# GpSimd's half of a weight split ahead of the seventh conditioning load, and 64-row products of attention in pairs on two row groups

## The reference

```python
hh = modulate(rmsnorm(x, g_pre), m[0], m[1])
f = swiglu(hh, w_ffn_gate, w_ffn_up, w_ffn_down)
x = x + 0.5 * m[2] * rmsnorm(f, g_post)
```

```python
att = einsum('bihd,bjhd->bhij', qb, kb) * decay
inner = einsum('bhij,bjhv->bihv', att, vb)
cross = einsum('bihd,bhdv->bihv', qb, s) * q_dec
s = s * c_dec + einsum('bjhd,bjhv->bhdv', kb * k_dec, vb)
```

## Time and profile before

| | before |
|---|---|
| time, median of 3 runs | 1464.51 us (1463.76 to 1464.62) |
| the profiled execution's own time | 1461.46 us |
| its span | 1459.8 us |
| PE busy | 1375.6 us, 94% of the span |
| DVE busy | 811.1 us, 56% |
| ACT busy | 611.9 us, 42% |
| POOL busy | 87.5 us, 6% |
| the chain that ended last, by engine | PE 82%, DVE 10%, ACT 3%, DMA 3%, issue 1% |
| TensorE's granted clock, mean | 0.973 of 2.4 GHz |

### The profile page before, as it was taken

The page is one execution under the profiler, slowest core; times in us unless marked ns, Lnnn a source line. Parts: engine busy times, 40 slices in busy tenths (PEclk is TensorE's granted clock), DMA queues, the critical chain, the costliest instruction groups (busy, mean ns, idle before and its releaser), DMA issues.

```text
span 1459.8 us, 24400 instructions
## 1 busy us (share of the span) xinstructions
PE 1375.6 (94%) x9782; PEld 1269.6 (87%) x9782; DVE 811.1 (56%) x1493; ACT 611.9 (42%) x1038; POOL 87.5 (6%) x139
## 2 busy tenths in 40 slices
PE   5899999989999998999999899999989798999996
PEld 1799999979886697999999799999979488999996
DVE  1544444577686677444445744445577877444434
ACT  2533333443332454333444433344445664334332
POOL 0000000013001101000000100000010200000000
PEclk8899999999998999999999999999999699999998
DMA  9565655456357665564345556434464733444342
GB/s 363 190 211 194 202 185 179 159 165 222 107 195 271 236 216 201 175 204 152 127 145 181 197 179 202 154 126 145 154 240 140 262 119 116 154 153 149 120 146 88
DMA packets 82196, 260.07 MB, mean 178 GB/s; under 512 B 11571, under 2 KB 22899, under 8 KB 81971
## 3 DMA queue, kind: packets, MB, share of 16 engines
q1 hardware_dynamic: 65618, 199.56, 41.3%
q0 software_dynamic: 16480, 59.15, 11.7%
HBM read 254.45 MB, written 4.23 MB: 177 GB/s over the span
## 4 chain that ended last, share of the span: by engine, by line
PE 82%; DVE 10%; ACT 3%; DMA 3%; issue 1%; SPq 0%; POOL 0%; DVEq 0%; ACTq 0%
PE ps L1492 25%; PE ps L1493 24%; PE ps L1494 24%; PE ps L1554 3%; DVE x L2006 1%; DMA a_raw<-in_ada 1%; DVE w_lo L1938 1%; DVE f L2020 1%; DVE f L2026 1%; DMA x<-in_x 1%; DVE f L2002 1%; PE ps L1576 1%; DVE xn_lo L2014 1%; DMA st_in<-in_state_ret 1%; PE ps L584 1%
## 5 line engine op out<-in xcount | busy, mean ns | idle before, releaser
L1492 PE MATMUL ps<-xn_hi,w_hi 128*128 128x320 f32 x1872 | 595.0, 318 | 34.7 <-DVE xn_lo L2014 25.3
L1493 PE MATMUL ps<-xn_lo,w_hi 128*128 128x320 f32 x1872 | 582.7, 311 | 0.0
L1494 PE MATMUL ps<-xn_hi,w_lo 128*128 128x320 f32 x1872 | 582.6, 311 | 0.0
L1938 DVE TENSOR_TENSOR w_lo<-w_raw,w_hi 128x1024 fp32r<-128x1024 f32 (+1 forms) x357 | 382.0, 1110 | 129.5 <-ACT w_hi L1747 129.0
L1492 PEld LDWEIGHTS ps<-xn_hi,w_hi 128*128 128x128 f32 x1872 | 355.3, 190 | 63.3 <-issue 44.3
L1747 ACT ACTIVATE w_hi<-w_raw 128x1024 fp32r<-128x1024 f32 x362 | 331.1, 961 | 84.0 <-PE ps L1494 76.0
L1493 PEld LDWEIGHTS ps<-xn_lo,w_hi 128*128 128x128 f32 x1872 | 355.9, 190 | 1.2
L1494 PEld LDWEIGHTS ps<-xn_hi,w_lo 128*128 128x128 f32 x1872 | 355.4, 190 | 0.0
L1492 PE MATMUL ps<-mid_hi,w_hi 128*128 128x320 f32 x704 | 218.2, 310 | 0.3 <-DVE w_lo L1938 0.3
L1493 PE MATMUL ps<-mid_lo,w_hi 128*128 128x320 f32 x704 | 217.1, 308 | 0.0
L1494 PE MATMUL ps<-mid_hi,w_lo 128*128 128x320 f32 x704 | 217.1, 308 | 0.0
(11 more groups left out here) (274 smaller groups left out, 901.1 us busy)
## 6 DMA issues: line engine op xcount, KB each, us to landing
w_raw<-in_gu SPq DMA_DIRECT2D x176, 512.0 KB, 4.8
a_raw<-in_ada POOLq DMA_DIRECT2D x96, 512.0 KB, 5.6
w_raw<-in_down SPq DMA_DIRECT2D x64, 512.0 KB, 3.6
w_raw<-in_pj SPq DMA_DIRECT2D x58, 512.0 KB, 4.9
w_raw<-in_down SPq DMA_DIRECT2D x64, 192.0 KB, 3.6
a_raw<-in_ada SPq DMA_DIRECT2D x16, 512.0 KB, 8.0
w_raw<-in_ada SPq DMA_DIRECT2D x16, 512.0 KB, 7.5
lent_hi<-in_ada SPq DMA_DIRECT2D x8, 512.0 KB, 9.2
```

Of the source, the lines that this page charges most:

```text
L1492: pe.matmul(out, hi, xhi, start=start, stop=False)
L1493: pe.matmul(out, hi, xlo, start=False, stop=False)
L1494: return pe.matmul(out, w_lo[s][:, w_at:w_at + P], xhi, start=False, stop=stop)
L1938: dve.tensor_tensor(w_lo[s][:, cols], w_raw[:, s, cols], w_hi[s][:, cols].bitcast(F32), ALU.subtract).then_inc(w_split, 1)
```

## The change

Two edits that have nothing to do with each other.

In `boundary`, `low_ahead` is called ahead of the load of piece seven; pieces seven and eight are then loaded together. Nothing else of the boundary changes.

In attention, products of 64 rows are put in pairs on the two halves of the partitions. `logits` of a prompt unit writes key head 0 to bank 4 and key head 1 to bank 5, without `lg_row`, and waits until the unit before has been read (`lg_ready` u, where it was u - 1). `spread` gives the 64 sample tokens of k and v a second time, on partitions 64 to 127, by a product with the identity (one more for k and one for v in each head). `kt` and `vt` are copied on 128 partitions. `vm` is 128 partitions by 4x128: sequences 0 to 3 on the lower half, 4 to 7 on the upper. The two products of 512 columns then take their rows from one half each. The tables `kdec` and `bmask` follow.

```diff
--- before.py
+++ after.py
@@ -213,7 +213,7 @@
         am_s = rb("am_s", [STOK, STOK])
         s1 = rb("s1", [P, P])
         s2 = rb("s2", [P, P])
-        vm = rb("vm", [STOK, NB, P])
+        vm = rb("vm", [P, NB // 2, P])
         under.close()
         xn_hi = sb("xn_hi", [P, KC, TOK], F32R)
         xn_lo = sb("xn_lo", [P, KC, TOK], F32R)
@@ -314,7 +314,7 @@
         dec_p = pb("dec_p", [P, RH, P])
         dec_s = pb("dec_s", [STOK, RH, STOK])
         kdec = pb("kdec", [P, 2, RH])
-        bmask = pb("bmask", [STOK, NB])
+        bmask = pb("bmask", [P, NB // 2])
         ones_h = pb("ones_h", [P, P])
         stack.close()
         ropet, rope_a, rope_b = f[:, 0:4, :], f[:, 4:6, :], f[:, 6:8, :]
@@ -454,7 +454,7 @@
 
         vw_tr, vw_ready = sem("vw_tr"), sem("vw_ready")
         qiz_ready, wis_mm, wis_ready = sem("qiz_ready"), sem("wis_mm"), sem("wis_ready")
-        ix_row, lg_row = sem("ix_row"), sem("lg_row")
+        ix_row = sem("ix_row")
         ix_done = sem("ix_done")
         relu_ready = sem("relu_ready")
         relu_used = sem("relu_used")
@@ -497,7 +497,7 @@
 
             nk = unit_keys(u)
             if UNITS[u][0] == "p":
-                return ps[:, 4 + u % 2, 0:NKV * nk].rearrange("p (g n) -> p g n", g=NKV)
+                return ps[:, 4:6, 0:nk]
             first = 4 if u == N_PU else 0
             return ps[:, first:first + 2, 0:nk]
 
@@ -518,9 +518,8 @@
 
             pieces = pieces_of(stage)[0:KC]
             ada_load(gp, pieces[loaded:A_SLOTS])
-            ada_load(gp, pieces[A_SLOTS:A_SLOTS + 1])
             low_ahead(gp, stage, 0)
-            ada_load(gp, pieces[A_SLOTS + 1:KC])
+            ada_load(gp, pieces[A_SLOTS:KC])
 
         def ada_load(gp, pieces):
 
@@ -685,6 +684,8 @@
                 for bank, src, done in ((0, rk, tr_k), (1, rv, tr_v)):
                     for c, (c0, n) in enumerate(CHUNKS):
                         last = pe.transpose(ps[0:n, bank, c * P:(c + 1) * P], src[:, c0:c0 + n], ident[:, :])
+                    last = pe.matmul(ps[STOK:P, bank, 2 * P:3 * P], src[:, PTOK:TOK], ident[:, :], start=True,
+                                     stop=True)
                     last.then_inc(done, 1)
                 for c in range(2):
                     pe.matmul(ps[:, 2, c * P:(c + 1) * P], rk[:, c * P:(c + 1) * P], rq[:, c * P:(c + 1) * P],
@@ -716,8 +717,9 @@
                 pe.matmul(ps[:, 3, P:2 * P], s1[:, :], qd[:, :], start=False, stop=True)
                 pe.wait_ge(vm_ready, h + 1)
                 for i in range(2):
-                    last = pe.matmul(ps[:, i, :], kt[0:STOK, 2, :],
-                                     vm[:, 4 * i:4 * i + 4, :].rearrange("p b v -> p (b v)"), start=True, stop=True)
+                    own = slice(STOK * i, STOK * (i + 1))
+                    last = pe.matmul(ps[:, i, :], kt[own, 2, :], vm[own, :, :].rearrange("p b v -> p (b v)"),
+                                     start=True, stop=True)
                 last.then_inc(kvs_done, 1)
 
             def cross(h):
@@ -732,8 +734,8 @@
             def logits(u):
                 kind, a, j = UNITS[u]
                 out_ = logit_banks(u)
-                if kind == "p" and u >= 2:
-                    pe.wait_ge(lg_ready, u - 1)
+                if kind == "p" and u:
+                    pe.wait_ge(lg_ready, u)
                 elif u == N_PU:
                     pe.wait_ge(lg_ready, u)
                 elif u == N_PU + 1:
@@ -741,13 +743,8 @@
                 for g in range(NKV):
                     rows = slice(HD * g, HD * (g + 1))
                     if kind == "p":
-                        if g:
-                            pe.wait_ge(lg_row, lg_n[0])
                         last = pe.matmul(out_[:, g, :], proj[rows, B_Q + j, P * a:P * (a + 1)],
                                          proj[rows, B_K, 0:unit_keys(u)], start=True, stop=True)
-                        if g == 0:
-                            last.then_inc(lg_row, 1)
-                            lg_n[0] += 1
                         continue
                     for b4 in range(4):
                         b = 4 * a + b4
@@ -757,8 +754,6 @@
                         last = pe.matmul(out_[out, g, PAST:KEYS_S], qb, proj[rows, B_K, PTOK:TOK],
                                          start=True, stop=True)
                 last.then_inc(lg_done, 1)
-
-            lg_n = [0]
 
             def turn(u):
 
@@ -885,8 +880,8 @@
                     act.wait_ge(kvs_done, h)
                 act.activation(kt[:, 0:2, :], ps[:, 0, 0:2 * P].rearrange("p (c n) -> p c n", c=2), ACT.Copy,
                                scale=kdec[:, 0, h:h + 1])
-                act.activation(kt[0:STOK, 2, :], ps[0:STOK, 0, 2 * P:3 * P], ACT.Copy,
-                               scale=kdec[0:STOK, 1, h:h + 1]).then_inc(kt_ready, 1)
+                act.activation(kt[:, 2, :], ps[:, 0, 2 * P:3 * P], ACT.Copy,
+                               scale=kdec[:, 1, h:h + 1]).then_inc(kt_ready, 1)
 
             def exponents(u):
                 act.wait_ge(lg_ready, u + 1)
@@ -1067,7 +1062,7 @@
                 if h:
                     dve.wait_ge(o_done, h)
                 dve.tensor_copy(vt[:, 0:2, :], ps[:, 1, 0:2 * P].rearrange("p (c n) -> p c n", c=2))
-                dve.tensor_copy(vt[0:STOK, 2, :], ps[0:STOK, 1, 2 * P:3 * P]).then_inc(vt_ready, 1)
+                dve.tensor_copy(vt[:, 2, :], ps[:, 1, 2 * P:3 * P]).then_inc(vt_ready, 1)
                 dve.tensor_tensor(qd[:, :], proj[:, RQ[h], P:2 * P], qdec[:, h, 0:P], ALU.mult)
                 dve.tensor_tensor(qz[:, :].rearrange("p (b w) -> p b w", b=NB)[:, :, 0:NT],
                                   tokens(proj[:, RQ[h], PTOK:TOK]), tokens(qdec[:, h, P:P + STOK]), ALU.mult)\
@@ -1149,8 +1144,8 @@
                 dve.wait_ge(vt_ready, h + 1)
                 if h:
                     dve.wait_ge(kvs_done, h)
-                dve.tensor_tensor(vm[:, :, :], vt[0:STOK, 2, :].unsqueeze(1).to_broadcast([STOK, NB, P]),
-                                  bmask[:, :].unsqueeze(2).to_broadcast([STOK, NB, P]), ALU.mult)\
+                dve.tensor_tensor(vm[:, :, :], vt[:, 2, :].unsqueeze(1).to_broadcast([P, NB // 2, P]),
+                                  bmask[:, :].unsqueeze(2).to_broadcast([P, NB // 2, P]), ALU.mult)\
                    .then_inc(vm_ready, 1)
                 soft(2 * h + 1)
                 if h < 2:
@@ -2345,9 +2340,9 @@
     out["qdec"] = np.broadcast_to(np.exp((step[None, P:] + 1.0) * lg[:, None]), (P, RH, P + STOK))
     kd = np.zeros((P, 2, RH))
     kd[:, 0] = np.exp((P - 1.0 - i[:, None]) * lg[None, :])
-    kd[0:STOK, 1] = np.exp((NT - 1.0 - tok[:, None]) * lg[None, :])
+    kd[:, 1] = np.exp((NT - 1.0 - np.tile(tok, 2)[:, None]) * lg[None, :])
     out["kdec"] = kd
-    out["bmask"] = (own[:, None] == np.arange(NB)[None, :])
+    out["bmask"] = np.concatenate([own[:, None] == 4 * i + np.arange(4)[None, :] for i in range(2)])
 
     q = np.arange(PTOK).reshape(2, P)
     out["bias_p"] = np.where(np.arange(PTOK)[None, None, :] <= q[:, :, None], 0.0, NEG).transpose(1, 0, 2)
```

## The result

| | before | after |
|---|---|---|
| median | 1462.52 us (1457.79 to 1465.15, 9 runs) | 1448.69 us (1445.59 to 1453.67, 9 runs) |
| the profiled execution's span | 1459.8 us | 1447.8 us |
| PE busy | 1375.6 us | 1366.2 us |
| DVE busy | 811.1 us | 800.3 us |

The ratio is 0.9905, 95% interval 0.989 to 0.992: 13.8 us less, where 15.1 were forecast. In a later set, on one chip with the experiments, the same pair gave 1448.91 against 1464.89 us, 0.99 (0.9879 to 0.9922). The forecast of 1449.4 us was made from a median of 1464.51.

A forecast was written before the change was run, and what follows sets the result against it. PE was taken as the bound, busy 94% of the span, with the gain in the chain's other 18%. Boundaries 9.1, eighth piece 1.1 and attention 4.9 sum to 15.1 us: 1464.51 to 1449.4 us, range 1445 to 1457.

The forecast's parts named there:

- the forecast case: Whole kernel: both edits gain, 15.1 us in all, to 1449.4 us; chance 0.56.
- The boundary additions: Five norm boundaries: DVE's additions fall to 0.48 us each once POOL's half runs ahead of them; 9.1 us gained.
- Piece eight: At odd_in: the eighth conditioning piece, loaded earlier, no longer keeps PE waiting 2.48 us; 1.1 us gained, ends 0 and 2.5.
- The 1.36 us for DVE: At odd_in: a PE wait for DVE, as seen in gate2, returns once the 2.48 us wait goes.
- Logits in pairs: Attention, prompt logits: second product starts at once; 0.69 us each in units 4 to 7, 2.8 us, plus 0.4 in unit 2.
- that wait for unit 2: Attention, unit 2: of 0.48 us only 0.4 counted, since the copy of the probabilities is late next.
- State products: Attention, heads 2 and 3: both products run at once, halving 1.91 us; 0.9 us each, 1.8 gained.
- vm: Head 1's chain through DVE: 512 columns instead of 1024, 1.12 us halved; 0.56 us gained.
- The products with the identity: Attention, two in each head: 0.1 us each, six on the path, 0.6 us lost; ends 0 and 1.4.
- Lent pieces: Heads 2 and 3: rival that these loads become the bound, 2 us in each; about 1453.3 us, chance 0.13 shared with serial row halves.
- The other victim: Boundaries: rival that POOL's moved half holds DVE's earlier steps instead, 0.6 us lost in each of five; 1462.6 us, chance 0.05.
- Half the clock through heads 2 and 3: Rival that TensorE's granted clock stays at 1.2 GHz there, up to 28 us more; 1477 us, chance 0.03.

The follow-up runs named there:

- bound_only: The boundary edit alone, attention as in the kernel before; 1451.86 us, 0.9909 of the kernel before.
- half_last: Against the changed kernel, both loads (seven, eight) put ahead of GpSimd's half; 1461.68 us, 0.9993 of the kernel before.
- attn_only: The attention edit alone, the boundaries as in the kernel before; 1459.98 us, 0.9974 of the kernel before.
- logits_only: Boundary edit plus paired logits; state products, vm and copies as before, no product with the identity; 1449.91 us, 0.9902 of the kernel before.

## Why the prediction was right, and where it was not

The time was right to 0.7 us (1448.69 for 1449.4), the gain was 13.8 us for 15.1, and the forecast case was the one that came. Step by step:

- **The boundary additions: right.** 9.06 us for 9.1, boundary by boundary within 0.02 us of 1.84, 1.87, 1.75, 1.77, 1.87; nothing came back later. bound_only and half_last show that the overlap is the cause.
- **Piece eight: right in kind, a chance in size.** The forecast of 1.1 lies between what four traces with a late piece lost: 1.4, 3.05, 2.2 and 0. The 1.36 us for DVE came back as forecast. What the forecast left out was the clock behind the wait: in the earlier trace rows the eight records after it took 1.08 us, where attn_only's took 0.64.
- **Logits in pairs: mechanism right, size too large.** I counted 0.69 us for each of units 4 to 7, 1.38 in a head. In logits_only PE got 0.74 and 0.56 and gave 0.42 back, waiting for DVE's probabilities: heads 2 to 3 came 0.84 us closer. I had named that wait for unit 2 and not for the others.
- **State products: right**, 1.06 us for 1.91. vm: 0.60 for 1.12 in head 1's chain, as forecast; but that chain as a whole grew from 10.33 to 10.88 us, because the products with the identity stand ahead of it.
- **The products with the identity: the step that failed.** "I take 0.1" each, with an upper end of 0.24, priced from the widths of products; they cost 0.485, and slow the next group by 0.1 us. In three heads that is 3.2 us for 0.6, beyond the end of 1.4. The nearest row, the two column groups of L788, showed products of one width among themselves and not the border to another width. With it the second pairing is worth nothing (logits_only), and the attention edit alone gives 3.8 us (1.8 to 5.9) where 4.9 were forecast, which the interval does not exclude; heads 2 and 3 are 15.46 us apart, not 14.2.
- **The sum came out better than its parts, and that is luck.** Where the clock is the same or nearly so, the attention edit shows some 1.8 us of the 4.9. What was missed was in part made up by the clock: in the first pair of traces head 0 to head 1 went from 20.27 to 17.36 us and head 1 to head 2 from 16.04 to 17.22, and no term of the sum stands for either.
- **The rivals.** Lent pieces did not become the bound: no wait for one shows. The other victim did not appear: L1997 kept 0.46 to 0.49 us. Half the clock through heads 2 and 3 did not come; the granted clock was 1.00 from 465 to 490 us in every trace. That the clock decides a few us around the waits, before and after the change, was not among the cases, and should have been.

## What to carry to other kernels

Before an operation on a helper engine is called free, look at what the others do in the same microseconds: 2.4 us of GpSimd in SBUF stretched one 0.48 us addition of DVE to its own length, five times, and moving the helper by 2.5 us gave 9 of the 14 us. When products are put side by side on parts of the array, price the borders too. Here each border between operands of 64 and 128 columns cost about 0.1 us of PE, and products widened to 128 columns, the surplus thrown away, did not pay it; in the whole time no run could tell the difference. A gain beside a wait, behind which the granted clock may be low, should be looked for in several traces of each kernel, since one trace here differed from the next of the same kernel by more than the edit brought.

## What was not expected of the hardware

- A product with a 64-column operand among operations on 128 columns starts 0.20 us after its neighbour instead of 0.11, and so does the one after it; a transpose of 64 tokens does not.
- Additions whose records begin 0.03 to 0.15 us ahead of GpSimd's operation were still held for the whole of it (2.76 to 2.89 us).
- The length of PE's wait does not tell what the clock does next. At odd_in the wait of 1.59 us left it at its level, and those of 2.48, 2.75 and 3.32 us were followed by 4 us at a mean of 0.57, 0.57 and 0.68. But behind the 2.0 us after head 3 the traces show both, and so they do behind the 0.96 and the 1.50 us in head 1.
